# First block's merge and gated FFN: plain fp32 matmuls in place of three passes on rounded parts, with four weight slots

## The reference, cut to what matters

```python
y_a = gelu_y * sigmoid(gelu_y @ w_glu)                          # 1024 x 1024
merged = (sigmoid(p[..., o5:o6]) * (y_a @ w_ssm_proj)           # 1024 x 1024
          + sigmoid(p[..., o6:]) * (y_b @ w_hgrn_proj))         # 1024 x 1024
h = h + merged @ w_out                                          # 1024 x 1024
z = rmsnorm(h, ffn_norm_g)
u = causal_dwconv(z @ w_up, conv_w, conv_b)                     # 1024 x 5632, 3 taps
h = h + (silu(u[..., :2816]) * u[..., 2816:]) @ w_down          # 2816 x 1024
```

## Time and profile before

| | us |
|---|---|
| Time, median of 3 runs | 2683.72 |
| the three runs | 2677.67, 2683.72, 2685.01 |
| Span of the profiled execution | 2677.4 |
| PE busy in it | 2456.7 (92%) |
| DVE busy, ACT busy | 1181.2 (44%), 735.2 (27%) |
| Stage merge, first to last matmul | 553.1 to 739.4 |
| Stage ffn, up projection | 745.5 to 1001.3 |
| Stage ffn, down projection | 1001.3 to 1128.3 |
| Stage moe, first expert matmul | 1744.1 |

### The profile page before, as it was taken

The page is one execution under the profiler, slowest core; times in us unless marked ns, Lnnn a source line. Parts: engine busy times, 40 slices in busy tenths (PEclk is TensorE's granted clock), DMA queues, the critical chain, the costliest instruction groups (busy, mean ns, idle before and its releaser), DMA issues. The chain is left out here.

```text
span 2677.4 us, 45140 instructions
## 1 busy us (share of the span) xinstructions
PE 2456.7 (92%) x19448; PEld 1721.8 (64%) x19448; DVE 1181.2 (44%) x1949; ACT 735.2 (27%) x1175; POOL 130.2 (5%) x142
## 2 busy tenths in 40 slices
PE   8998878989999999999989989799898988899888
PEld 7998667789999997777767757533333333333232
DVE  6775656644556663366655576411111111111113
ACT  4221264433333432253323174310000000000001
POOL 1000022100000000003200030100000000000000
PEclk9999989999999999999999999899999999999999
DMA  5444451345422213333323226599999999999997
GB/s 166 139 129 117 96 188 59 120 166 180 127 101 88 90 70 117 105 118 130 128 89 93 80 93 212 217 410 430 431 431 431 430 431 431 430 431 431 430 430 290
DMA packets 154598, 608.10 MB, mean 227 GB/s; under 512 B 50144, under 2 KB 71776, under 8 KB 129376
## 3 DMA queue, kind: packets, MB, share of 16 engines
q1 hardware_dynamic: 127792, 574.53, 55.1%
q10 hardware_dynamic: 26608, 30.68, 3.7%
HBM read 565.86 MB, written 36.95 MB: 225 GB/s over the span
## 5 line engine op out<-in xcount | busy, mean ns | idle before, releaser
L3888 PE MATMUL moe_bank<-moe_ring,xg 128*64 128x512 f32 x2048 | 490.4, 622 | 88.1 <-DMA moe_ring<-in_w_exp_up 87.3
L3888 PEld LDWEIGHTS moe_bank<-moe_ring,xg 128*64 128x64 f32 x2048 | 154.6, 142 | 366.2 <-issue 357.3
L4178 DVE TENSOR_TENSOR moe_sg<-moe_sg,moe_bank 64x512 f32<-64x512 f32 x64 | 44.1, 690 | 576.5 <-ACT moe_sg L4046 576.5
L3918 PE MATMUL moe_bank<-moe_ring,moe_act_t 128*64 128x512 f32 x1008 | 227.0, 592 | 0.0
L68 PE MATMUL ffn_prod<-ffn_x_low,ffn_w_high 128*128 128x258 f32 x704 | 200.0, 284 | 5.8 <-PEq L138 5.8
L68 PE MATMUL in_bank<-x_low,in_w_high 128*128 128x264 f32 x640 | 185.8, 290 | 16.9 <-DVE in_w_low L1011 9.2
L69 PE MATMUL ffn_prod<-ffn_x_high,ffn_w_low 128*128 128x258 f32 x704 | 200.0, 284 | 0.0
L70 PE MATMUL ffn_prod<-ffn_x_high,ffn_w_high 128*128 128x258 f32 x704 | 199.1, 283 | 0.0
L70 PE MATMUL in_bank<-x_high,in_w_high 128*128 128x264 f32 x640 | 184.0, 287 | 0.0
L69 PE MATMUL in_bank<-x_high,in_w_low 128*128 128x264 f32 x640 | 183.5, 287 | 0.0
L3918 PEld LDWEIGHTS moe_bank<-moe_ring,moe_act_t 128*64 128x64 f32 x1008 | 72.2, 137 | 143.5 <-issue 143.5
(11 more groups left out here) (597 smaller groups left out, 5060.9 us busy)
## 6 DMA issues: line engine op xcount, KB each, us to landing
moe_ring<-in_w_exp_gate SPq DMA_DIRECT2D x64, 2048.0 KB, 27.6
moe_ring<-in_w_exp_up SPq DMA_DIRECT2D x64, 2048.0 KB, 21.3
moe_ring<-in_w_exp_down SPq DMA_DIRECT2D x63, 2048.0 KB, 25.8
rw_w<-in_w_in SPq DMA_DIRECT2D x48, 512.0 KB, 3.4
ffn_w<-in_w_up SPq DMA_DIRECT2D x44, 512.0 KB, 4.1
in_w<-in_w_in SPq DMA_DIRECT2D x40, 512.0 KB, 3.9
ffn_w<-in_w_down SPq DMA_DIRECT2D x16, 704.0 KB, 4.0
p<-in_out ACTq DMA_DIRECT2D x32, 264.0 KB, 4.0
```

The lines of the kernel that those rows point to most:

```text
L3888: last = nc.tensor.matmul(bank[64 * g:64 * g + 64, s], xe[:, (e // BATCH) % 2, k, at:at + CAPACITY], ring[:, slot_of(n, g), k * HALF:(k + ...
L3918: last = nc.tensor.matmul(bank[64 * h:64 * h + 64, 3 + e % 2], act_t[:, s, j], weights[:, at:at + HALF], start=(c == 0 and j == 0), stop=( ...
L4178: nc.vector.tensor_tensor(sg[0:CAPACITY, s], sg[0:CAPACITY, s], bank[64:64 + CAPACITY, s], ALU.mult).then_inc(act_ready, 1)
```

## The change

In `project_chain` and `conv_gated_ffn` `three_passes` is gone. One matmul per tile takes the fp32 operands as they are. With the parts go their casts, subtractions, buffers and semaphores. The weights get four slots in place of two (in merge: slots of 1 MB; in ffn: pairs of tiles), each loaded again when the matmuls on it are done. Hgrn loads all four first slots of `w_glu` (4 MB in place of 1 MB) and no longer splits one. `h` stays in SBUF as the residual and is neither stored nor loaded again. The first weights of "front" are loaded earlier, but the second of their casts waits for the last down product, and VectorE subtracts both behind the last output tile.

```diff
 # project_chain, SyncE
-                    if g >= 3:
-                        sp.wait_ge(w_ready, g - 2)
+                for g in range(slots_w, len(slots)):
+                    n, j = slots[g]
+                    sp.wait_ge(y_ready, g - slots_w + 1)
...
+                    if g >= 2 * per_step:
+                        load_e(g - 2)
+                    if g == 2 * per_step - 1:
+                        sp.wait_ge(res_ready, per_step)
+                        for k in range(KT):
+                            sp.dma_start(x_first[:, k], steps[2][3][k * P:(k + 1) * P, :]).then_inc(x_loaded[k], 16)
 # project_chain, TensorE
-                        if j == 0 and (m, h) == (0, 0):
-                            pe.wait_ge(x_ready, x_before[n] + k + 1)
-                        done = three_passes(nc, y[:, s, m, h, 0:w_t], w_high[:, s, k, columns],
-                                            w_low[:, s, k, columns], x_highs[n % 2][:, k, tokens],
-                                            x_lows[n % 2][:, k, tokens], k == 0, k == kts[n] - 1)
+                            if n in (1, 3):
+                                pe.wait_ge(res_ready, per_step * (n - 1) + k // nm + 1)
+                            elif n == 2:
+                                pe.wait_ge(x_loaded[k], 16)
+                        done = nc.tensor.matmul(y[:, s, m, b, 0:w_t], w[:, g % slots_w, k, m * P:(m + 1) * P],
+                                                operands[n][:, k, b * w_t:(b + 1) * w_t], start=(k == 0), stop=(k == KT - 1))
 # conv_gated_ffn, TensorE
-                                done = three_passes(nc, prod[:, s, g, h, 0:hw], w_high[:, s, g, k], w_low[:, s, g, k],
-                                                    x_high[:, k, tokens], x_low[:, k, tokens], k == 0, k == kt - 1)
+                                done = nc.tensor.matmul(prod[:, s, g, b, 0:hw], w[:, t % SLOTS, g, k], x[:, k, b * hw:(b + 1) * hw],
+                                                        start=(k == 0), stop=(k == kt - 1))
...
-                        done = three_passes(nc, prod[:, m % 2, 0, 0, 0:TO], high[:, columns], low[:, columns],
-                                            a_high[:, k, first:], a_low[:, k, first:], k == 0, k == FT - 1)
+                        done = nc.tensor.matmul(prod[:, m % 2, 0, 0, 0:TO], weights[:, i * P:(i + 1) * P], a[:, k, first:],
+                                                start=(k == 0), stop=(k == FT - 1))
 # conv_gated_ffn, ScalarE and VectorE, at the end
-                act.wait_ge(prod_ready, items - 1)
                 for n in range(2):
+                    act.wait_ge(prod_ready, items - 1 + n)
                     nc.scalar.copy(first_high[:, n], first_w[:, n]).then_inc(first_high_ready, 1)
...
-                    nc.vector.tensor_tensor(h[:, m], prod[:, m % 2, 0, 0, 0:TO], res_of(m), ALU.add).then_inc(out_ready, 1)
+                    nc.vector.tensor_tensor(h[:, m, first:], prod[:, m % 2, 0, 0, 0:TO], h[:, m, first:], ALU.add).then_inc(out_ready, 1)
+                for n in range(2):
+                    dve.wait_ge(first_high_ready, n + 1)
+                    nc.vector.tensor_tensor(first_low[:, n], first_w[:, n], first_high[:, n].bitcast(F32),
+                                            ALU.subtract).then_inc(first_low_ready, 1)
 # two_blocks, the loads that hgrn issues for merge
-            next_loads = [(merge_w[:, 0], d["ssm_w_glu"].rearrange("(k p) m -> p k m", p=P)[:, :, 0:2 * P])] + [
-                (x_first[:, k], ya_kept[k * P:(k + 1) * P, :]) for k in range(KT)]
+            next_loads = [(merge_w[:, j], w_glu[:, :, 2 * P * j:2 * P * (j + 1)]) for j in range(4)]
+            next_loads[1:1] = [(x_first[:, k], ya_kept[k * P:(k + 1) * P, :]) for k in range(KT)]
```

More of the change, by code:

```diff
@@ L82, in project_chain @@
     per_step = D_MODEL // width
-    halves = 1 if T <= 512 else 2
-    w_t = T // halves
+    slots_w = w.shape[1]
+    halves, w_t = 2, T // 2
     slots = [(n, j) for n in range(len(steps)) for j in range(per_step)]
-    kts = [w.shape[0] // P for _, w, *_ in steps]
-    x_before = [sum(kts[:n]) for n in range(len(steps))]
-    assert all(steps[n][0] is not None or steps[n - 1][4] == "x" for n in range(len(steps)))
+    operands = (x_first, x_next, x_first, merged)
     with ExitStack() as ctx:
         sb, ps, sem = opener(nc, ctx, stage)
-        x_highs = x_high, sb("x_high", [P, KT, T], F32R)
-        x_lows = x_low, sb("x_low", [P, KT, T], F32R)
         gate = sb("gate", [P, 2, nm, T])
@@ L123, in tiles, with e_loads @@
             return slice(nm * j, nm * j + nm)
[L125 to L136, removed]
+        def e_loads(g):
+            return 16 * ((g - per_step) // 2 + 1)
         with nc.Block() as block:
@@ L199, in _ @@
-                for k in range(kts[0]):
-                    split_x_high(0, k)
                 for g, (n, j) in enumerate(slots):
                     s = g % 2
-                    _, _, epilogue, _, goes_to = steps[n]
-                    if g + 1 < len(slots):
-                        split_w_high(g + 1)
-                    if j == 1 and n + 1 < len(steps) and steps[n + 1][0] is not None:
-                        for k in range(kts[n + 1]):
-                            split_x_high(n + 1, k)
-                    if epilogue != "add":
+                    epilogue = steps[n][1]
@@ L227, in _ @@
+                        nc.scalar.activation(flat(gate[:, s]), y_of(s), ACT.Sigmoid).then_inc(gate_ready, 1)
+                    elif epilogue != "add":
+                        act.wait_ge(res_ready, g - 1)
+                        act.wait_ge(e_loaded[s], e_loads(g))
+                        nc.scalar.activation(gate[:, s], e[:, s], ACT.Sigmoid).then_inc(gate_ready, 1)
+                    else:
+                        act.wait_ge(res_ready, g + 1)
                         if j == 0:
                             act.wait_ge(gain_loaded, 16)
-                            act.wait_ge(y_ready, per_step * n)
@@ L276, in _ @@
                     elif epilogue == "gate":
-                        nc.vector.tensor_tensor(flat(to), y_of(s), flat(gate[:, s]), ALU.mult).then_inc(res_ready, 1)
+                        nc.vector.tensor_tensor(flat(merged[:, tiles(j)]), y_of(s), flat(gate[:, s]), ALU.mult).then_inc(res_ready, 1)
                     elif epilogue == "gate_add":
                         nc.vector.tensor_tensor(flat(gate[:, s]), y_of(s), flat(gate[:, s]), ALU.mult).then_inc(gated, 1)
-                        dve.wait_ge(gated, sum(steps[i][2] == "gate_add" for i, _ in slots[:g + 1]))
+                        dve.wait_ge(gated, j + 1)
@@ L290, in _ @@
[L290 to L294 removed]
+                        dve.wait_ge(e_loaded[s], e_loads(g))
+                        nc.vector.tensor_tensor(flat(h[:, tiles(j)]), y_of(s), flat(e[:, s]), ALU.add).then_inc(res_ready, 1)
@@ L437, in _ @@
                             pe.wait_ge(out_ready, m - 1)
-                    high, low = piece_of(w_high, n % 2), piece_of(w_low, n % 2)
+                    weights = piece_of(n)
                     for i in range(PIECE_K):
```

334 lines of the change are left out of this document (84 added, 250 removed).

## The result

| | before | after |
|---|---|---|
| Median, us | 2684.36 (4 runs, 2677.67 to 2686.52) | 2799.86 (4 runs, 2799.43 to 2811.1) |
| Profiled execution: span, us | 2677.4 | 2809.2 |
| Its mean granted clock | 0.972 | 0.968 |

After is to before as 1.0447 to 1, with a 95% interval of 1.0425 to 1.047. By the medians that is +115.5 us, where +119.8 was forecast: 2799.9 us against 2803, inside the range of 2789 to 2832.

What follows compares the result with a forecast made beforehand. TensorE was taken to bound merge and ffn, with split work and loads hidden beside it. Products +121.7, waits gone -4.5 and -0.7, new waits +2.3 and +1.0 gave +119.8 us: 2803 us, range 2789 to 2832.

Steps and rivals of the forecast that it cites:

- merge, products: Merge's matmuls: 1024 plain records of 0.218 us, 223.2 us in place of 184.8, +38.4 us.
- up, products: Up projection's matmuls: 1408 plain records of 0.218 us, 306.9 us in place of 252.3, +54.6 us.
- down, products less its wait: Down projection: products +28.7 us; the wait for split weights and the half clock behind it go, -4.5.
- start of merge: Merge's first matmul no longer needs a split: -0.7 us, or -1.4 if the clock also rises earlier.
- between merge and ffn: Gap between these stages: the chain of add, square and two sums stays, so nothing, at most 0.5 us won.
- end of hgrn: Hgrn's last part: 3 MB more loads ahead of the gate stores delay them; +1 us, bounds -1 and +4.5.
- start of front: VectorE adds first and subtracts behind, so the barrier falls later; TensorE idles 3.4 us, not 1.05: +2.3 us.
- 12 to 19 ns more for each record: Rival on merge and ffn matmuls: changing weights cost what an F32R pass pays, total 2832 us; 8%.
- The 0.09 us behind L2413: Rival on merge and ffn matmuls: a weight load exposed once a matmul, +125 us, total 2929 us; 3%.
- a plain product two passes long: Rival on merge and ffn: plain fp32 takes two passes, not four, so the change wins, about 2461 us; 2%.
- The waits that go: TensorE waits expected to vanish: down projection -4.5 us, merge's first matmul -0.7, nothing between merge and ffn.
- the -1 for the split: Lower bound at hgrn's end: -1 us if the split on VectorE (L1744, 2.28 us) was the only delay.

Runs made afterwards that it cites:

- e1: Kernel before with only the three matmuls of each merge and ffn tile product replaced by one plain fp32 matmul on the high parts; 2797.71 us, ratio 1.0432.
- e4: Kernel before with each residual load in the down projection issued behind the next weight load in SyncE's queue; 2676.48 us, ratio 0.9977.
- e2: Changed kernel with hgrn's three extra 1 MB weight loads issued behind the first of the last three gate stores; 2796.5 us, ratio 1.0427.
- e8: The changed kernel run once more, unedited, on one chip with two mended kernels; 2796.94 us, ratio 1.0417 to before.
- e5: Kernel before without the low-weights pass in merge and ffn, so two passes, all casts and subtractions kept; 2567.96 us, ratio 0.9571.
- e7: Kernel before, three passes, with seven of eight matmuls of each merge and up sum on 128 columns only; 2696.93 us, one run.
- e6: Changed kernel with seven of eight matmuls of each merge and up sum on 128 columns only; 2579.64 us, one run.

## Why the prediction was right, step by step

| step | predicted, us | measured, us |
|---|---|---|
| merge, products | +38.4 | +39.2 |
| up, products | +54.6 | +54.4 |
| down, products less its wait | +28.7 - 4.5 = +24.2 | +24.1 |
| start of merge | -0.7 | -1.4 |
| between merge and ffn | 0 (at most -0.5) | -0.7 |
| end of hgrn | +1.0 (-1 to +4.5) | +2.9 |
| start of front | +2.3 | +2.2 |
| sum | +119.8 | +120.7 |

**The products.** They carry 117.7 of the 120.7 us, so the forecast was right by its mechanism. That the sums agree to within 1 us is in part luck: the end of hgrn cost 1.9 us more than forecast, and the next two gaps 1.4 us less. The pace was taken at 0.218 and 0.4295 us a record and came out at 0.2175 and 0.430. With the half clock taken out of both sides (the first 3.0 us of merge in before, 4.9 in after, 556.76 to 561.7), merge is 184.8 and 223.1 us, +38.3. The start of merge won 1.4 us and merge lost 0.8 to the clock; the prediction had counted both together as -0.7. The condition that a product of 258 columns takes 0.43 to 0.445 us holds (0.435). What made this step safe was that the trace of before held the new operation in its very shape, and another with changing weights. The 0.275 us that the prediction takes for a record there is the median of a row that mixes 128 and 16 columns, so its surplus of 1 to 5 ns was less sure than it looked; after measures 2.5 ns on 258 columns. One reading was wrong and harmless: a weight slot lasts 32 tile products, 13.9 us, and not 28.

**The rivals on the pace.** 12 to 19 ns more for each record, as F32R shows them, would be a pace of 0.2275; it isn't there. The 0.09 us behind L2413 is not paid at a change of weights between full tiles either. Why it is paid at L2413, where the row layout changes too, stays open and was not tried. Nor is a plain product two passes long: 704 products left 1408 records, each with the time of two passes over its columns. The Trainium skill (Perfetto Trace Analysis, Engine Utilization) halves the array's rate for FP32_LOW_HIGH; the trace agrees only for a single record, and a matmul has two. The rule of the Trainium skill that a weight load overlaps matmuls only when it goes to other row groups (TensorE: Matmul & The Clock Gate, Part 3, The mechanism) is contradicted here: all tiles use all rows, and a record of 0.2175 us beside the 0.215 of two passes over its columns has no room for an exposed load. The same section also lets a load go ahead into a background weight buffer, which would fit; no run here shows which it is.

**The waits that go.** The down projection's wait went and its half clock with it, and the sum of -4.5 fits. The prediction gave as the reason that a piece now waits only for a load. That was only partly right: e1 shows that the longer products would have covered it with the split left in, and e4 that it was no matter of the split by itself, since the piece's weights came late behind a load that waited. The first matmul of merge stands 0.04 us behind the stage's first queue entry, as forecast.

**The end of hgrn.** This is the mis-sized term. The prediction named the mechanism, loads ahead of the gate stores, and bounded it, but then took +1 where +2.9 came. From the first 16-column transpose to the last there are 8.05 us (545.62 to 553.67) in place of 5.18 (543.45 to 548.63), and e2 has 4.00. The first gap, in which TensorE waits for `hgrn_og`, shows the parts: 1.48 us in before, 4.13 in after, 0.65 in e2. So the loads ahead of the gate store cost 3.5 us, and the split that goes from VectorE's list (L1744) gives back 0.8. The remaining +0.2 lies in the later transposes, which after runs wholly at half the clock. The prediction had the -1 for the split nearly right, which with its +1 leaves about 2 us for the wait for the store, where 3.5 was measured. By its own working the store would land at 543 to 549, 546 in the middle; it landed just before 549.03, which is 546.9 in the time of before, as this profile is 2.2 us late by then.

**What the sum does not hold.** Between the two profiles there are 131.8 us, 11 more than the steps. These lie in code that is the same in both: 2.2 us before the end of hgrn and 8.9 behind front's start. After had half the clock for 184.6 us in all, before for 153.9; the same kernel in e8 had it for 143.8 and a span of 2786.6. That is 22.6 us between two profiles of one kernel. Most of the difference in clock lies behind front's start, where after's mean granted clock is 0.96 and that of before and e8 0.97: half the clock for 123 us there against 96 and 93. The 27 us more can cost up to 14, which is enough for the 8.9. The medians (+113 to +117 us over after, e1, e2 and e8) come a little below the steps' +120.7. Such a difference between profiles is large enough for that, but why they all lie on this side isn't shown.

## What to carry to other kernels

Count passes times columns before trading one kind of matmul for another: here plain fp32 cost four passes (4 x 258 columns / 2.4 GHz = 0.430 us, 0.435 measured) against three of 0.1195 us, and the engines that it relieved had been hidden. The choice turns around on narrow tiles, where an F32R pass doesn't get below 0.11 us; and fewer passes help only until VectorE's list behind them, split work included, takes longer than they do, as in e5 with 56 us of new waits (10.3 us a pair against 7.7). In a queue that serves loads and stores in order, put a transfer that waits, or a large one that isn't needed yet, behind the small one that somebody is waiting for (3.3 us in e2, 4.5 us in e4's ffn).

## What the runs showed of the hardware beyond this

- **The floor under an F32R pass.** 0.111 us on 128 columns and 0.1195 on 258, both with new weights each time. A plain record on 128 columns, with two passes in it, takes 0.112.
- **A clock at half under unbroken work.** In e7 the granted clock stood at half, 1.2 GHz, from 547.2 to 639.4 us. TensorE was then busy without a gap from 560 to 630 us at least (70.00 of 70.00 us): 330 passes in 70 us are 0.212 us each, nearly twice the 0.112 of its window behind. The up projection of e7 then began with 12.4 us at half (773.6 to 786.0), where that of before had 5.2. In e6 the stretch from 565 to 680 us had the full clock. Nothing in these traces says why the clock rose at 639.4 and not earlier; it is one profile, and it was not repeated.
- **The same idle time, another clock.** 3.3 us of idle TensorE ahead of front were followed by half the clock in three profiles of four, about 1 us of it in none of eight.
- **An engine that is not full can set the pace.** In e5's up projection VectorE is busy for 158 of 220.7 us and TensorE for 183, and yet TensorE waits 19 times for VectorE's scaling, since VectorE's list for a pair takes 10.3 us with its own short waits.
